# Weight chunks of 128x1024 split in place, and every second modulation chunk multiplied on TensorE in one stage

## The chip, the cores and the metric

The kernel runs on one core of one Trainium2 chip. A core has TensorE (matrix multiplication, PE in the profile; its weight loads are PEld), VectorE (DVE), ScalarE (ACT), GpSimd (POOL) and SyncE (SP), which here only issues DMAs. The engines run side by side and meet at semaphores. The metric is device time in microseconds (us), the median of the runs; lower is better.

## The reference

Two transformer blocks in fp32 for 256 tokens with a width of 2048. Cut to what the change touches:

```python
c_act = silu(c)
mod = c_act @ ada_w + ada_b                   # (2048) @ (2048, 12288): six rows of 2048
sh1, sc1, g1, sh2, sc2, g2 = split(mod, 6)
u = rms_norm(h, norm_mix_g) * (1 + sc1) + sh1
h = h + g1 * hybrid_mixer(u, w_in, ..., w_out)
u = rms_norm(h, norm_ffn_g) * (1 + sc2) + sh2
h = h + g2 * ((silu(u @ w_gate) * (u @ w_up)) @ w_down)
h = rms_norm(h, final_norm_g)
# second block: two layers, each u = h @ w_in_2; pooling or attention; memory attention; @ w_out_2; layer_norm
```

Nearly all the time goes into products of 256 tokens with large weight matrices, and into `c_act @ ada_w`, a product of one row with 100 MB of weights.

## The kernel before

**Stages.** Weights are worked through in stages (`STAGES`, line 72): `memkv`, `ada1`, `win`, `win_end`, attention, `wout`, then `gu0`, `down0`, `gu1` and so on, `in0`, `out0`, `kv`, `in1`, `out1`. A stage has bodies (a loop) of panels. A panel is 512 columns of a matrix, and its 2048 rows are 16 blocks of 128 rows, fetched as 8 chunks of two blocks (512 KB). The kind of a panel says what it fetches: `w` a weight matrix, `a` a slice of `ada_w`, `wa` both in turn. `ada1` has four panels of kind `a`: it fetches only modulation weights, 32 chunks, and its results (shift and gain) are needed before `win` can begin, the first panel of which is of kind `w`.

**A weight block** must keep fp32 accuracy on TensorE, so it is split in two: ScalarE rounds it (`w_hi`, line 338), VectorE subtracts (`w_lo`, line 370), and TensorE does three matmuls of 512 columns for each half of the tokens (lines 444 to 446), 6 in a block, 12 in a chunk. `w_hi` and `w_lo` each have 4 slots of one block (`HILO`).

**A modulation block** is multiplied by its scalars of `c` and added up on VectorE: `ada_acc` = block x `c_col` + `ada_acc` (line 377 for the first block of a panel, 385 for the other 15). Each waits for the one before. When the 16 are done, TensorE adds up the 128 partitions with four fp32 matmuls of one column against `ones` (`ada_sum`, line 402; the profile records eight), and VectorE takes the four columns out of PSUM bank 6 and adds the bias (`take_columns`, line 1479). The take of a panel stands in VectorE's program at block 12 of the panel after it.

**The ring.** SyncE fetches into `raw`, 8 slots of one chunk (`RING`), in order, one DMA each (two in the `gu` stages). Before each fetch it waits for one counter, `blocks_read`, which VectorE raises once a block is subtracted or accumulated. So a slot is free as soon as VectorE has read it, while TensorE may still be up to four blocks behind. SyncE's waits stand in one queue: a fetch whose slot is not free holds up all behind it.

**Order of the other work.** Small steps are hooked into the programs of the engines at block numbers. At the start of some stages (a *lead*) the activations are turned by TensorE (line 483), and for each pair of blocks VectorE scales them (line 551 or 553, `evac`), ScalarE rounds (line 526), VectorE subtracts (line 558, `actT`), between the splits of the weights. In `kv`'s lead GpSimd scales `X` (lines 1080 and 1083, `natural`) beside that. In `wout` and the `down` stages VectorE's hook `gated_add` adds a finished panel to `X`.

Of the kernel before, what the change touches and what calls it, by code (L numbers as in the profile page):

```python
# [56 lines left out]
RING, HILO = 8, 4  # L57
# [6 lines left out]
class Stage:  # L64
# [8 lines left out]
    Stage("memkv", 2, [("wa", 16)] * 2), Stage("ada1", 2, [("a", 16)] * 2),  # L73
# [13 lines left out]

# [5 lines left out]
for _s in STAGES:  # L93
    _s.start = (_kb, _gb, _pn, _an)
    _s.local = []
    k = g = n = a = 0
    for _kind, _nk in _s.panels:
        _s.local.append((k, g, n, a))
        k += _nk * len(_kind)
        g += _nk * ("w" in _kind)  # L100
# [20 lines left out]
def program(nc, x, c, ada_w, ada_b, norm_mix_g, norm_ffn_g, w_in, fox_f_bias, cmp_w1, cmp_w2, cmp_pos,  # L121
# [6 lines left out]
    with ctx:  # L128
# [23 lines left out]
        r_hilo = region(2 * HILO * NC * 4)  # L152
        w_hi = at("w_hi", [P, HILO, NC], f32r, r_hilo)
        w_lo = at("w_lo", [P, HILO, NC], f32r, r_hilo + HILO * NC * 4)
# [95 lines left out]
        blocks_read = S("blocks_read")  # L250
        hi_ready = S("hi_ready")
        parts_used = S("parts_used")
# [5 lines left out]
        def chunks(stage, j):  # L258
# [3 lines left out]
            for ch in range(nk // 2):  # L262
                for k in kind:
                    yield k, ch, off
                    off += 2

        def stage_loads(sp, name, w_src, a_src=None, width=NC):
            st = ST[name]

            def body(p, first):  # L270
                for j in range(len(st.panels)):
                    pl = place(st, p, j)
                    for kind, ch, off in chunks(st, j):
                        slot = ((st.start[0] + st.local[j][0] + off) // 2) % RING

                        sp.wait_ge(blocks_read, pl.kb + off + 2)
# [10 lines left out]
        for st in STAGES:  # L287
# [3 lines left out]
            for j in range(len(st.panels)):  # L291
                row = []
                for kind, ch, off in chunks(st, j):
                    s = ((st.start[0] + st.local[j][0] + off) // 2) % RING
# [18 lines left out]
        def stage_split_hi(act, name, hooks=None, width=None, lead=None):  # L313
# [3 lines left out]
            def body(p, first):  # L317
                for j in range(len(st.panels)):
# [4 lines left out]
                    for idx, (kind, ch, off) in enumerate(chunks(st, j)):  # L323
                        if kind != "w":
                            continue
                        for b in range(2):
                            k = 2 * ch + b
# [4 lines left out]
                            if b == 0:  # L332
                                wait_chunk(act, st, p, j, idx)
                            slot = ((st.start[0] + st.local[j][0] + off) // 2) % RING

                            act.wait_ge(parts_used, pl.gb + k + 1)
                            g = (st.local[j][1] + k) % HILO
                            act.activation(w_hi[:, g, 0:w], raw[:, slot, b, 0:w], ACT.Copy).then_inc(hi_ready, 1)  # L338
            run_bodies(act, st, body)

        def stage_split_lo(dve, name, hooks=None, width=None, take=None, one_acc=False, lead=None):
# [7 lines left out]
            def body(p, first):  # L349
                na = 0  # L350
                for j in range(len(st.panels)):
# [3 lines left out]
                    for idx, (kind, ch, off) in enumerate(chunks(st, j)):  # L355
                        slot = ((st.start[0] + st.local[j][0] + off) // 2) % RING
                        for b in range(2):
                            k = 2 * ch + b
# [7 lines left out]
                            if kind == "w":  # L366

                                dve.wait_ge(hi_ready, pl.gb + k + 1)
                                g = (st.local[j][1] + k) % HILO
                                nc.vector.tensor_tensor(w_lo[:, g, 0:w], raw[:, slot, b, 0:w],  # L370
                                                        w_hi[:, g, 0:w].bitcast(f32),
                                                        ALU.subtract).then_inc(blocks_read, 1)
                            else:
                                acc = ada_acc[:, 0 if one_acc else na % 2, :]
                                if k == 0:
                                    wait_chunk(dve, st, p, j, idx)
                                    nc.vector.tensor_scalar(acc, raw[:, slot, b, :], c_col[:, 0:1], None,
                                                            ALU.mult).then_inc(blocks_read, 1)
                                else:
                                    if b == 0:  # L380
                                        wait_chunk(dve, st, p, j, idx)
# [1488 lines left out]
```

## Time and profile before

| | us |
|---|---|
| median of 3 runs | 2327.52 |
| lowest and highest | 2325.42, 2329.5 |
| span of the profiled execution | 2324.9 |
| TensorE busy | 2105.9 (91%) |
| VectorE busy | 1503.5 (65%) |
| ScalarE busy | 1063.4 (46%) |
| DMA, mean | 209 GB/s |

The profiled execution has its span of 2324.9 us only; what lies around it is the 2.6 us to the median. An x with a number is a count of instructions. A bracket at the end of a row of a timeline tells how long the engine was idle before it, and what released it. PEclk is the clock that TensorE was granted, 1.00 for 2.4 GHz and 0.50 for 1.2 GHz.

### The profile page before, as it was taken

The numbers are of one execution on the slowest core, as the hardware profiler recorded it, in microseconds if no ns is written. First come the engines' busy times: TensorE is split into PE (matmuls) and PEld (weight loads), VectorE is DVE, ScalarE is ACT, GpSimd is POOL, SyncE is SP. The second block draws the span as 40 slices with busy tenths as digits, with TensorE's granted clock in tenths as the row PEclk, the third lists the DMA queues.
The fourth block names the chain that finished last, engine by engine and source line by source line (L and its number), as shares of the span: only waits on it lengthen the run. The fifth ranks groups of instructions, "written<-read, shape, count | busy, mean of one in ns | idle before, by whom it ended". The sixth has DMA issues, their size and how long they took to land.

```text
span 2324.9 us, 29571 instructions
## 1 busy us (share of the span) xinstructions
PE 2105.9 (91%) x9820; PEld 1731.4 (74%) x9820; DVE 1503.5 (65%) x2632; ACT 1063.4 (46%) x1931; POOL 117.8 (5%) x188
## 2 busy tenths in 40 slices
PE   6928999998798999999999999799799699999797
PEld 4817888776576887888888888588578578888675
DVE  5988888656898877555555556755345755555466
ACT  3414444466334544445544554455334445555542
POOL 2000000221003000000000000100000300000000
PEclk9958999999899999999999999899899899999998
DMA  9986998523796997666656665466526356664462
GB/s 299 387 297 230 359 320 312 172 80 89 278 335 203 293 292 244 199 191 190 189 188 194 190 189 186 132 196 193 166 78 226 109 168 194 190 197 138 154 218 99
DMA packets 321589, 486.09 MB, mean 209 GB/s; under 512 B 33696, under 2 KB 145536, under 8 KB 320064
## 3 DMA queue, kind: packets, MB, share of 16 engines
q1 hardware_dynamic: 318704, 468.63, 62.6%
q0 software_dynamic: 2768, 15.98, 1.9%
q8 instruction: 64, 1.05, 0.2%
q14 instruction: 53, 0.43, 0.1%
HBM read 465.13 MB, written 2.10 MB: 201 GB/s over the span
## 4 chain that ended last, share of the span: by engine, by line
PE 75%; DVE 11%; issue 6%; SPq 3%; DMA 2%; ACT 2%; POOL 0%; DVEq 0%; POOLq 0%; ACTq 0%
PE ps L444 23%; PE ps L446 23%; PE ps L445 23%; DVE ada_acc L385 4%; SPq L812 3%; DVE w_lo L370 3%; PE ps L483 1%; PE ps L696 1%; PE ps L659 1%; ACT w_hi L338 1%; DMA raw<-in_w_mem_kv 1%; PE ps L1311 1%; PE ps L643 1%; DVE evac L551 1%; DMA raw<-in_w_out 1%
## 5 line engine op out<-in xcount | busy, mean ns | idle before, releaser
L370 DVE TENSOR_TENSOR w_lo<-raw,w_hi 128x512 fp32r<-128x512 f32 (+1 forms) x1328 | 919.1, 703 | 628.4 <-ACT w_hi L338 626.2
L338 ACT ACTIVATE w_hi<-raw 128x512 fp32r<-128x512 f32 (+1 forms) x1328 | 829.4, 629 | 1004.4 <-PE ps L446 893.0
L444 PE MATMUL ps<-w_hi,actT 128*128 128x512 f32 (+1 forms) x2304 | 915.1, 397 | 60.3 <-DVE actT L558 24.4
L446 PE MATMUL ps<-w_hi,actT 128*128 128x512 f32 (+1 forms) x2304 | 901.7, 391 | 0.0
L445 PE MATMUL ps<-w_lo,actT 128*128 128x512 f32 (+1 forms) x2304 | 901.2, 391 | 0.0
L444 PEld LDWEIGHTS ps<-w_hi,actT 128*128 128x128 f32 x2304 | 437.4, 190 | 162.2 <-DVE actT L558 27.9
L446 PEld LDWEIGHTS ps<-w_hi,actT 128*128 128x128 f32 x2304 | 437.0, 190 | 92.1
L445 PEld LDWEIGHTS ps<-w_lo,actT 128*128 128x128 f32 x2304 | 438.3, 190 | 88.5 <-issue 1.4
L385 DVE SCALAR_TENSOR_TENSOR ada_acc<-raw,c_col,ada_acc 128x512 f32<-128x512 f32 x360 | 271.7, 755 | 11.7 <-DMA raw<-in_ada_w 2.3
L444 PE MATMUL ps<-w_hi,hidT 128*128 128x512 f32 x352 | 137.7, 391 | 2.8 <-DVE w_lo L370 2.8
L446 PE MATMUL ps<-w_hi,hidT 128*128 128x512 f32 x352 | 137.0, 389 | 0.0
L445 PE MATMUL ps<-w_lo,hidT 128*128 128x512 f32 x352 | 137.0, 389 | 0.0
L444 PEld LDWEIGHTS ps<-w_hi,hidT 128*128 128x128 f32 x352 | 66.1, 188 | 18.5 <-DVE w_lo L370 2.6
L446 PEld LDWEIGHTS ps<-w_hi,hidT 128*128 128x128 f32 x352 | 66.1, 188 | 13.9
L445 PEld LDWEIGHTS ps<-w_lo,hidT 128*128 128x128 f32 x352 | 66.1, 188 | 13.4
L402 PE MATMUL ps<-ones,ada_acc 128*128 128x1 f32 x128 | 18.8, 268 | 51.1 <-DVE ada_acc L385 51.1
L696 PE MATMUL ps<-v_s,probsT 128*128 128x64 f32 (+1 forms) x424 | 56.2, 282 | 9.3 <-DVE probsT L788 7.8
L696 PEld LDWEIGHTS ps<-v_s,probsT 128*128 128x128 f32 x424 | 52.7, 198 | 11.7 <-DVE probsT L788 8.6
L402 PEld LDWEIGHTS ps<-ones,ada_acc 128*128 128x128 f32 x128 | 19.6, 225 | 52.3 <-DVE ada_acc L385 51.5
L659 PE MATMUL ps<-qkT_s 64*128 64x256 f32 (+3 forms) x272 | 46.2, 389 | 11.2 <-ACT probs L726 6.1
L726 ACT ACTIVATE probs<-probs,sm 128x128 f32<-128x128 f32 x120 | 52.8, 444 | 4.4 <-DVE sm L776 4.4
L1074 POOL TENSOR_TENSOR rinv_x<-ms,mhalf 128x2 f32<-128x2 f32 x4 | 3.4, 854 | 994.7 <-DVE ms L1511 916.6
(212 smaller groups left out, 1056.6 us busy)
## 6 DMA issues: line engine op xcount, KB each, us to landing
raw<-in_w_in SPq DMA_DIRECT2D x216, 512.0 KB, 4.1
raw<-in_ada_w SPq DMA_DIRECT2D x192, 512.0 KB, 5.6
raw<-in_w_out SPq DMA_DIRECT2D x96, 512.0 KB, 4.9
raw<-in_ffn_w_gate SPq DMA_DIRECT2D x176, 256.0 KB, 2.9
raw<-in_ffn_w_up SPq DMA_DIRECT2D x176, 256.0 KB, 3.1
raw<-in_ffn_w_down SPq DMA_DIRECT2D x88, 512.0 KB, 4.1
raw<-in_w_kv_shared SPq DMA_DIRECT2D x48, 512.0 KB, 3.7
raw<-in_w_mem_kv SPq DMA_DIRECT2D x32, 512.0 KB, 8.8
```

The costliest lines, as they stand in the source:

```text
L338: act.activation(w_hi[:, g, 0:w], raw[:, slot, b, 0:w], ACT.Copy).then_inc(hi_ready, 1)
L370: nc.vector.tensor_tensor(w_lo[:, g, 0:w], raw[:, slot, b, 0:w], w_hi[:, g, 0:w].bitcast(f32), ALU.subtract).then_inc(blocks_read, 1)
L385: nc.vector.scalar_tensor_tensor(acc, raw[:, slot, b, :], c_col[:, k:k + 1], acc, ALU.mult, ALU.add).then_inc(blocks_read, 1)
L402: last = nc.tensor.matmul(ps[:, 6, i:i + 1], acc[:, i * P:(i + 1) * P], ones[:, 0:1], start=True, stop=True)
L444: nc.tensor.matmul(o, hi, w_hi[:, g, 0:w], start=(k == 0), stop=False)
L445: nc.tensor.matmul(o, hi, w_lo[:, g, 0:w], start=False, stop=False)
L446: last = nc.tensor.matmul(o, lo, w_hi[:, g, 0:w], start=False, stop=(k == nk - 1))
L483: last = nc.tensor.transpose(ps[:, 4 + g % 4, i * P:(i + 1) * P], src(k, t), ident[:, :])
L659: last = nc.tensor.matmul(ps[:, 2 + h, c0:c0 + nk], q[:, t * P:(t + 1) * P], k[:, 0:nk], start=True, stop=True)
L696: last = nc.tensor.matmul(o, probsT[:, par, h, d:d + P], self.v(par, h, kt), start=(kt == 0), stop=(kt == nk // P - 1))
L726: last = act.activation(probs[:, par, h, c0:c0 + nk], src, ACT.Exp, bias=sm[:, par, q:q + 1], scale=self.scale, accum_out=sm[:, par, 4 + q ...
L812: sp.dma_start(dst, src[:, t]).then_inc(sem, 16)
```

## The change

The splits are made for a whole chunk, 128x1024, with one instruction on ScalarE and one on VectorE, half as many as before. `w_lo` has no buffer of its own: it is written over the chunk in `raw`. `w_hi` gets the room, and holds 4 chunks (8 blocks) where it held 4 blocks. TensorE waits once in a chunk and frees it once, after its 12 matmuls.

`blocks_read` is replaced by three counters. SyncE now frees a slot by what was in it: a weight chunk when TensorE has done its matmuls (`parts_used`), a modulation chunk when VectorE has accumulated it (`ada_step`) or TensorE has multiplied it (`ada_pe`).

In `ada1` alone the panels become of kind `ap`: chunks 0, 2, 4, 6 go to VectorE as before, chunks 1, 3, 5, 7 to TensorE, where `ada_direct` multiplies the raw fp32 weights with a column of `c` into the four columns of bank 6: eight fp32 matmuls of one column in a chunk. `ada_sum` then adds VectorE's half to the same columns. Because these share the bank, `ada_direct` waits until the panel before was taken (`ada_taken`), and that take still stands in VectorE's program at block 12, so behind chunk 4 of the panel.

```diff
-RING, HILO = 8, 4
+RING, HI = 8, 4
...
-Stage("ada1", 2, [("a", 16)] * 2),
+Stage("ada1", 2, [("ap", 16)] * 2),
...
+        w_lo = at("w_lo", [P, RING, 2, NC], f32r, 0)
+        r_hilo = region(HI * 2 * NC * 4)
+        w_hi = at("w_hi", [P, HI, 2, NC], f32r, r_hilo)
...
+        def slot_free(sp, st, p, first, j, off):
+
+            per = st.per[0]
+            n = st.start[0] + st.local[j][0] + off - RING + (0 if first else per)
+            if n < 0:
+                return
+            kind = loaded[n]
...
+            if kind == "w":
+                sp.wait_ge(parts_used, HI + done)
+            elif kind == "a":
+                sp.wait_ge(ada_step, 2 * done)
+            else:
+                sp.wait_ge(ada_pe, done)
...
-                        sp.wait_ge(blocks_read, pl.kb + off + 2)
+                        slot_free(sp, st, p, first, j, off)
...
-                            act.wait_ge(parts_used, pl.gb + k + 1)
-                            g = (st.local[j][1] + k) % HILO
-                            act.activation(w_hi[:, g, 0:w], raw[:, slot, b, 0:w], ACT.Copy).then_inc(hi_ready, 1)
+                        act.wait_ge(parts_used, pl.gb + ch + 1)
+                        g = (st.local[j][1] + ch) % HI
+                        act.activation(w_hi[:, g, :, 0:w], raw[:, slot, :, 0:w], ACT.Copy).then_inc(hi_ready, 1)
...
+                            nc.vector.tensor_tensor(w_lo[:, slot, :, 0:w], raw[:, slot, :, 0:w],
+                                                    w_hi[:, g, :, 0:w].bitcast(f32),
+                                                    ALU.subtract).then_inc(lo_ready, 1)
...
+        def ada_direct(pe, st, p, j):
+
+            pl = place(st, p, j)
+            pe.wait_ge(ada_taken, pl.an + 1)
+            for idx, (kind, ch, off) in enumerate(chunks(st, j)):
+                if kind != "p":
+                    continue
+                wait_chunk(pe, st, p, j, idx)
+                slot = slot_of(st, j, off)
+                for b in range(2):
+                    k = 2 * ch + b
+                    for i in range(4):
+                        last = nc.tensor.matmul(ps[:, 6, i:i + 1], raw[:, slot, b, i * P:(i + 1) * P], c_col[:, k:k + 1],
+                                                start=(idx == 1 and b == 0 and i == 0), stop=False,
+                                                skip_group_check=True)
+                last.then_inc(ada_pe, 1)
...
+                            if b == 0:
+                                pe.wait_ge(lo_ready, pl.gb + ch + 1)
...
-                            last.then_inc(parts_used, 1)
+                        last.then_inc(parts_used, 1)
```

## Rows read from the trace of the kernel before

**Rows 1.** Busy time by stretch: engine us (x), PEclk, DMA share, GB/s

```profile
55.00:110.00 55.00, 55.00 (x251) 45.57 (x250) 52.45 (x82) 26.97 (x47) 0.00 (x0) 1.00 1.05 387
110.00:165.00 55.00, 16.73 (x82) 14.52 (x81) 47.86 (x76) 9.66 (x16) 1.36 (x2) 0.64 0.88 304
1155.00:1210.00 55.00, 55.00 (x248) 45.54 (x247) 29.70 (x46) 27.14 (x46) 0.00 (x0) 1.00 0.60 191
```

**Rows 2.** Waits: waiter <- waited for: us in total, times, longest

```profile
PE ps L402 <- DVE ada_acc L385: 51.1, 4, 18.7
PE ps L444 <- DVE w_lo L370: 20.4, 20, 3.3
ACT w_hi L338 <- PE ps L446: 893.0, 1155, 7.6
```

**Rows 3.** Timeline, VectorE, ada1: start us, length us, line, tiles, count

```profile
123.11 4.83 DVE L1501 BATCH_NORM_STATS2 stats<-X 128x6 f32<-128x512 f32 x8
129.38 12.25 DVE L385 SCALAR_TENSOR_TENSOR ada_acc<-raw,c_col,ada_acc 128x512 f32<-128x512 f32 x15
```

**Rows 4.** Timeline, TensorE, ada1 and the start of win

```profile
141.68 1.87 PE L402 MATMUL ps<-ones,ada_acc 128*128 128x1 f32 x8 [18.69 <-DVE ada_acc L385]
179.73 1.87 PE L402 MATMUL ps<-ones,ada_acc 128*128 128x1 f32 x8 [10.82 <-DVE ada_acc L385]
187.26 0.77 PE L444 MATMUL ps<-w_hi,actT 128*128 128x512 f32 x1 [1.71 <-issue]
```

**Rows 5.** Line 402 (min/median/max ns), and its eight records in memkv

```profile
L402 PE MATMUL ps<-ones,ada_acc x128: 165/250/373, 64.9 to 471.7; 128*128 128x1 f32 x128
87.61 0.95 PE L402 MATMUL ps<-ones,ada_acc 128*128 128x1 f32 x8
```

**Rows 6.** Thin matmuls in win_end (timeline), and granted clock around their end

```profile
401.27 4.07 PE L1235 MATMUL ps<-cmp_in,w_s 64*64 64x30 f32 x64
...
404.00:405.00 1.00, 1.00 (x20) 1.00 (x19) 0.00 (x0) 0.00 (x0) 0.00 (x0) 0.94 0.55 211
405.00:406.00 1.00, 1.00 (x6) 0.84 (x5) 0.00 (x0) 0.00 (x0) 0.00 (x0) 0.50 0.07 27
```

**Rows 7.** Timeline, memkv in steady state: queue, ScalarE, VectorE

```profile
88.78 1.29 DVE L370 TENSOR_TENSOR w_lo<-raw,w_hi 128x512 fp32r<-128x512 f32 x2
89.99 1.53 DVE L385 SCALAR_TENSOR_TENSOR ada_acc<-raw,c_col,ada_acc 128x512 f32<-128x512 f32 x2
90.10 0.37 SPq L279 DMA_DIRECT2D raw<-in_w_mem_kv  x1
90.82 1.24 ACT L338 ACTIVATE w_hi<-raw 128x512 fp32r<-128x512 f32 x2 [1.54 <-DMA raw<-in_w_mem_kv]
```

**Rows 8.** Page, DMA issues: count, KB each, us from issue to landing

```profile
raw<-in_ffn_w_down SPq DMA_DIRECT2D x88, 512.0 KB, 4.1
raw<-in_w_mem_kv SPq DMA_DIRECT2D x32, 512.0 KB, 8.8
```

**Rows 9.** Groups with shapes kept apart, VectorE

```profile
L1804 DVE TENSOR_TENSOR U<-U 128x1024 f32<-128x1024 f32 x1 | 1.2, 1224 | 0.0
```

**Rows 10.** Timeline, first panel of win: one group of the lead

```profile
199.76 1.29 DVE L370 TENSOR_TENSOR w_lo<-raw,w_hi 128x512 fp32r<-128x512 f32 x2 [0.62 <-ACT w_hi L338]
```

**Rows 11.** Timeline, first panel of kv: VectorE, GpSimd, TensorE

```profile
1844.15 9.84 DVE L370 TENSOR_TENSOR w_lo<-raw,w_hi 128x512 fp32r<-128x512 f32 x2 [0.62 <-ACT w_hi L338]
1848.62 4.82 POOL L1083 TENSOR_TENSOR X<-X,gb 128x2048 f32<-128x2048 f32 x1
1858.96 0.79 PE L444 MATMUL ps<-w_hi,actT 128*128 128x512 f32 x1 [12.35 <-DVE actT L558]
1866.04 0.79 PE L444 MATMUL ps<-w_hi,actT 128*128 128x512 f32 x1 [2.48 <-DVE actT L558]
```

**Rows 12.** Timeline, TensorE: starts of down0, and inside down2

```profile
912.29 0.47 PE L444 MATMUL ps<-w_hi,hidT 128*128 128x512 f32 x1 [1.47 <-DVE w_lo L370]
1426.22 0.50 PE L444 MATMUL ps<-w_hi,hidT 128*128 128x512 f32 x1 [0.45 <-DVE w_lo L370]
```

More of the change, by code:

```diff
@@ L72 @@
 STAGES = [
[L73 removed]
+    Stage("memkv", 2, [("wa", 16)] * 2), Stage("ada1", 2, [("ap", 16)] * 2),
     Stage("win", 2, [("w", 16)] + [("wa", 16)] * 3), Stage("win_end", 1, [("wa", 16), ("w", 16)] * 2),
@@ L262, in chunks, with slot_of @@
             for ch in range(nk // 2):
-                for k in kind:
+                for k in kind[ch % 2] if kind == "ap" else kind:
                     yield k, ch, off
-                    off += 2
+                    off += 1
+        def slot_of(st, j, off):
+            return (st.start[0] + st.local[j][0] + off) % RING
+        loaded = "".join(k for st in STAGES for _ in range(st.bodies)
+                         for j in range(len(st.panels)) for k, _, _ in chunks(st, j))
+        def slot_free(sp, st, p, first, j, off):
[4 more added lines that the diff above has]
+            kind = loaded[n]
+            done = loaded[:n + 1].count(kind)
+            each = sum(k == kind for j2 in range(len(st.panels)) for k, _, _ in chunks(st, j2))
+            done = done if first else done - each + p * each
+            if kind == "w":
[4 more added lines that the diff above has]
+                sp.wait_ge(ada_pe, done)
         def stage_loads(sp, name, w_src, a_src=None, width=NC):
@@ L355, in body @@
                     for idx, (kind, ch, off) in enumerate(chunks(st, j)):
-                        slot = ((st.start[0] + st.local[j][0] + off) // 2) % RING
-                        for b in range(2):
-                            k = 2 * ch + b
+                        slot = slot_of(st, j, off)
+                        for k in (2 * ch, 2 * ch + 1):
                             if not alone and kind == kinds[j][0]:
@@ L396, in ada_sum @@
             kind, nk = st.panels[j]
-            pe.wait_ge(blocks_read, 2 * RING + pl.kb + nk * len(kind))
+            pe.wait_ge(ada_step, steps_before(st, pl) + (KD // 2 if kind == "ap" else KD))
             pe.wait_ge(ada_taken, pl.an + 1)
-            if as_columns:
+            if kind == "ap":
+                for i in range(4):
+                    last = nc.tensor.matmul(ps[:, 6, i:i + 1], acc[:, i * P:(i + 1) * P], ones[:, 0:1],
+                                            start=False, stop=(i == 3), skip_group_check=True)
+            elif as_columns:
                 for i in range(4):
@@ L443, in body @@
                                 o = ps[:, bank + t, 0:w]
[L444 to L447 removed]
+                                nc.tensor.matmul(o, hi, w_hi[:, g, b, 0:w], start=(k == 0), stop=False)
+                                nc.tensor.matmul(o, hi, w_lo[:, slot, b, 0:w], start=False, stop=False)
+                                last = nc.tensor.matmul(o, lo, w_hi[:, g, b, 0:w], start=False, stop=(k == nk - 1))
+                        last.then_inc(parts_used, 1)
             run_bodies(pe, st, body)
```

79 lines of the change are left out of this document (38 added, 41 removed).

## The prediction

> **What bounds the kernel now.** I read busy time by stretch first, then the waits, then the timeline at the places that those name. In `memkv` (55 to 110) TensorE has no gap, at full clock; VectorE is busy for 52.45 of 55 us and the DMAs bring 387 GB/s, so three resources are nearly full together. In the stages of pure weights TensorE has no gap either, and VectorE (29.70) and the DMAs (191 GB/s) have room. From 110 to 165, mostly `ada1`, TensorE is busy for 16.73 us and VectorE for 47.86 [rows 1]. The waits say the same: TensorE's longest is in line 402 for `ada_acc`, 51.1 us in 4 waits; all its waits for `w_lo` come to 20.4 us [rows 2]. So the kernel is bound by TensorE's weight matmuls, except in `ada1`, where VectorE's chain of accumulations sets the end, and in some starts of stages.
>
> **`ada1` before.** VectorE first does the statistics of `x` (from 123.11), then the blocks one behind the other: 15 in 12.25 us, so 0.82 us each [rows 3]. The sums of the four panels stand from 141.68 to 179.73, so 12.68 us for a panel; the last one ends at 181.6, and `win`'s first matmul starts at 187.26 [rows 4].
>
> **`ada1` after: TensorE's chain.** VectorE's part halves: 8 x 0.82 = 6.5 us for a panel. TensorE gets four chunks of eight fp32 matmuls, each chunk twice the work of one sum. A sum of the same form (weights 128x128, one column) is eight records and takes 1.87 us here [rows 4], and 0.95 us in `memkv` [rows 5]; the difference is the clock. Which clock will `ada_direct` see? The nearest row is the run of thin matmuls in `win_end`: 64 records with 30 columns, back to back for 4.07 us, with TensorE counted busy for 1.00 of each us; the granted clock was still 0.94 in their last us and 0.50 in the next one, so that the dense matmuls behind them started at half clock [rows 6]. `ada_direct` has one column, and in front of three of its four panels the clock is low already. I take the low clock throughout, 1.2 GHz. Eight records one after the other take 1.71 us then (1.87 less the tail of the last one, which the next covers: longest record 373 ns [rows 5] less the spacing of 214), so a panel is 8 x 1.71 = 13.7 us, at most 8 x 1.87 = 15.0.
>
> These 13.7 us are in a ring of waits. `ada_direct` of panel j waits for the take of panel j-1; that take waits for the sum of j-1; the sum stands behind `ada_direct` of j-1. So the period is 13.7 + 1.9 (sum) + 0.3 (take, semaphores) = 15.9 us, against 12.68. VectorE and the loads fit under it: chunk 3's slot comes free halfway through `ada_direct` (7 us), chunk 4 lands some 5 us later, VectorE needs 1.6 us: 13.6 of the 15.9. The first panel overlaps with the statistics: TensorE starts it at 123.2 and has done by some 133, VectorE begins its half one block before 129.38 and finishes at 128.9 + 8 x 0.8 = 135.3. For the first take, VectorE must get through chunks 0, 2, 4 of panel 1, which the DMAs at 387 GB/s (1.36 us a chunk) bring by 139.0, so 139.0 + 1.6 + 0.3 = 140.9. Then three periods: the last sum ends at 140.9 + 3 x 15.9 - 0.3 = 188.3, against 181.6: **+6.7 us** (with 15.0 for the direct part: +10.6). Nothing hides it, since `win` needs the result. Behind this SyncE has `win`'s loads, which are due only at 190.
>
> **The larger split.** ScalarE and VectorE do the same elements. 128x1024 takes VectorE 1.224 us [rows 9]; the pair it replaces takes 1.21 from its start to the next instruction's [rows 7]; with the usual overlap of 0.08 the new one takes 1.14. That is 0.07 us in a chunk, of use only where VectorE is the last, in `wout` (32 chunks): -2 to 0; I set it against the ring below. But the first `w_lo` of a chunk now waits for a `w_hi` of twice the length. Where TensorE stands still for it (`down0`, 1.47 us [rows 12], and the starts of `memkv` and `win_end`) that adds 0.5 to 0.6 us each: **+1.6**. In the leads VectorE waits 0.62 us for `w_hi` in every group [rows 10], and this grows to 1.1, so a group takes 0.45 more; over five groups +2.2 at most. Against that, `w_hi` has room for chunk 2 and later ones without waiting for TensorE, which gives a lead of 1 to 2.7 us at its beginning. I take **0** for the leads, -1 to +1.5 for each of four.
>
> **The deeper `w_hi`.** ScalarE waits 893.0 us for TensorE [rows 2]: it is early nearly always, and can now run four chunks ahead. In the stages of pure weights VectorE's hook is then covered: three stalls of 0.45 in `down2` (one in [rows 12]) go, **-1.4**. From 0 to -8 for the rest of the waits for `w_lo` [rows 2]; those in `wout` I expect to stay, since there VectorE or the DMAs are the bound.
>
> **GpSimd beside `kv`'s lead.** Two subtractions take 9.84 us together at 1844.15 and end as GpSimd's long instructions end (1848.62 starts the second); TensorE stands still for 12.35 and later 2.48 us [rows 11]. By these rows each VectorE instruction with two SBUF inputs waits for a boundary on GpSimd. One subtraction in place of two waits for one boundary fewer (4.8 us), but GpSimd's last boundary (1848.62 and three instructions of 4.9, so 1863.3) stays: the chunk after the 2.48 us stall can start at 1863.3 and not at 1866.04: **-2.7**, between -5 and 0. The Trainium skill (SBUF — State Buffer, "SBUF: two separate sides") calls the port pair of the two engines an exclusive lock held for the whole instruction. By that rule fewer and longer instructions lose fewer turns, which agrees with the row.
>
> **Slots freed later.** A `w` slot was freed when `w_lo` was written (90.10 follows 88.78 + 1.29 directly [rows 7]); now it stays until TensorE has done the chunk, at least 2.7 us more, and the modulation fetch behind it in SyncE's queue waits too. Of the four `w` slots in a `wa` panel each goes round once in 4 x 2.72 = 10.9 us: load + `w_hi` 1.2 + `w_lo` 1.2 + matmuls 2.7 + semaphores 0.3 = load + 5.4. It holds if a load takes up to 5.5 us. Loads take 4.1 us where the DMAs have room, 8.8 in `memkv` [rows 8], where six of them queue; fewer in flight also land sooner. Two fetches issued together give about 4.1 + 1.36 = 5.5, just the limit. Bounds 0 and +27 (8.8 us in 32 chunks: (14.2 - 10.9) / 4 = 0.83 each); I take +1, nearest to 4.1, and with the faster VectorE **0**.
>
> **Sum.** +6.7 + 1.6 - 1.4 - 2.7 + 0 = +4.2 us. The profiled span of 2324.9 becomes 2329.1, and with the 2.6 us around it the median of 2327.5 becomes 2331.7: **2332 us**.
>
> **A rule against it, and the rivals.** The Trainium skill (TensorE: Matmul & The Clock Gate, "Why this matters for your kernels") advises to keep TensorE busy without gaps to get and keep the full clock. By this rule the direct matmuls, which leave no gap, bring it to full clock; the thin matmuls of `win_end` speak against it.
>
> *Rival 1, the full clock in `ada1`* (22%). A chunk takes 16 x 0.12 = 1.9 us, a panel 7.6, a sum 0.95 [rows 5]. TensorE's ring is then 8.9 us, and the loads bind: 8 x 1.36 = 10.8, some 11 us for a panel. The first panel after the statistics has a low start (9.5 us), so the last sum ends near 172.4: -9.2 in place of +6.7. The start of `win`, at half clock now, saves 2.4 us as well. 4.2 - 15.9 - 2.4 = -14: 2313 us.
>
> *Rival 2, the ring starves* (13%), slower. It decides from a load of 5.5 us on: then `wa` stages run at the pace of the ring, with TensorE waiting for `w_lo` and ScalarE for DMAs. Up to +27 in `memkv`; half of it gives 2345.
>
> *Rival 3, the queue absorbs more* (10%): half of the 20.4 us of waits for `w_lo` goes: 2332 - 10 = 2322.
>
> *Rival 4, the engines don't share `ada1`*: that is within my forecast, since the take at block 12 makes TensorE wait for chunk 4 of the next panel.
>
> **How the numbers follow.** The forecast has 55%, with 2326 to 2339 as its own range (direct part of 15.0 us, GpSimd at 0, leads). Cases of both signs are likely, so the range reaches to rivals 1 and 2: 2311 to 2345. A measurement of this kernel can tell about 0.2% from no change, 4.7 us. Faster: rival 1 (21), rival 3 (6), the forecast's edge (3): 30%. Within: half of the forecast, and 4 of rival 3: 31%. Slower: the rest, 39%.
>
> **What would show it.** In the profile after: PEclk of 0.5 through `ada1`, sums 15.9 us apart, eight thin records in 1.7 us, first matmul of `win` near 194. In `memkv` still 12 matmuls in 2.72 us without gaps and w loads of 5 to 6 us. In `kv`'s lead one stall of TensorE shorter by 3 to 5 us. The forecast is wrong if the clock is high in `ada1`, or if TensorE waits for `w_lo` in `wa` panels.

## The result, and the profile after

| | before | changed |
|---|---|---|
| median of the runs, us | 2327.99 | 2345.74 |
| ratio | 1 | 1.0079, 95% interval 1.006 to 1.0098 |
| the same measured again | 2323.74 | 2341.87, ratio 1.0067, 1.005 to 1.0084 |
| span of the profiled execution | 2324.9 | 2344.8 (again: 2341.9) |

The change costs about 18 us (17.75 and 18.13 between the medians). 2332 was forecast, and 2345.74 lies just outside the range of 2311 to 2345. The four times behind it reach from 2336.14 to 2347.37, and the second measurement, 2341.87, lies inside the range; so what counts is not the edge but the size of the loss, four times the forecast +4.2.

To see where a loss arises I cut the profiled executions at marks that every kernel has: TensorE's first weight matmul, the sums of `ada_sum`, the turning of the activations. The stretches, each the difference of two starts in TensorE's timeline (us):

| | to the first matmul | `memkv`: to its last sum | `ada1`: to its last sum | `win`, attention: to the turning for `wout` | `wout`: to the turning of `xn` | to `kv`'s turning | to the end | span |
|---|---|---|---|---|---|---|---|---|
| before | 27.5 | 94.5 | 57.7 | 414.1 | 127.2 | 1105.2 | 498.6 | 2324.9 |
| changed | 29.0 | 103.1 | 65.0 | 411.7 | 130.3 | 1108.7 | 497.0 | 2344.8 |
| changed, again | 28.6 | 101.7 | 65.2 | 415.4 | 127.9 | 1106.4 | 496.7 | 2341.9 |

Two stages carry the loss: `memkv` with 7.2 to 8.6 us and `ada1` with 7.3 to 7.5.

**`memkv`.** Busy time by stretch, changed kernel; columns as in [rows 1]:

```profile
core 0: us, PE busy (x) PEld busy (x) DVE busy (x) ACT busy (x) POOL busy (x), PEclk, DMA share, GB/s
55.00:110.00 55.00, 49.60 (x216) 40.46 (x215) 46.81 (x57) 21.02 (x22) 0.00 (x0) 0.94 0.99 354
1155.00:1210.00 55.00, 55.00 (x249) 45.54 (x248) 24.80 (x26) 20.66 (x25) 0.00 (x0) 1.00 0.60 190
```

Against [rows 1], TensorE and VectorE have lost their full use (5.4 us of gaps, 5.6 us less of VectorE's work), and the DMAs bring 354 in place of 387 GB/s. None of the engines is full there any more: they wait for one another. The stages of pure weights are as full as before, with less work on VectorE (24.80 in place of 29.70) and ScalarE. The waits of the changed kernel (waiter <- waited for: us in total, times, longest), to be read beside [rows 2]:

```profile
PE ps L496 <- DVE w_lo L389: 24.6, 15, 4.7
ACT w_hi L358 <- PE ps L498: 530.8, 348, 5.7
ACT w_hi L358 <- DMA raw<-in_w_mem_kv: 72.2, 32, 11.9
DVE ada_acc L404 <- DMA raw<-in_ada_w: 24.2, 17, 4.5
```

ScalarE waited 42.0 us for the `memkv` weights before and waits 72.2 now. The one long stall, in the timelines of SyncE's queue, ScalarE and TensorE (start, length, ..., idle before it and what ended it):

```profile
55.26 0.37 SPq L301 DMA_DIRECT2D raw<-in_w_mem_kv  x1
57.87 0.37 SPq L303 DMA_DIRECT2D raw<-in_ada_w  x1
65.16 0.37 SPq L301 DMA_DIRECT2D raw<-in_w_mem_kv  x1
57.47 1.06 ACT L358 ACTIVATE w_hi<-raw 128x1024 fp32r<-128x1024 f32 x1 [7.62 <-DMA raw<-in_w_mem_kv]
59.92 0.77 PE L496 MATMUL ps<-w_hi,actT 128*128 128x512 f32 x1 [4.70 <-DVE w_lo L389]
```

A chunk arrives late, TensorE stands still for 4.70 us, and since a weight slot is freed by TensorE now, SyncE issues nothing from 57.87 to 65.16. That pause itself makes no second stall: the chunk issued at 65.16 lands at 68.8, and TensorE reaches it at 74.0. What the stall costs beside its own length is the clock: it falls to 0.50 meanwhile (rows in the last section), so that the 12 matmuls behind it take 5.05 us in place of 2.72. Those 2.3 us, the 4.70 and two later gaps (0.70 and 0.36) are 8.1 of the 8.6 us. What made the chunk late shows in the DMAs' view of 44 to 60 us (out<-in, queue, count, KB each, median us from issue to landing):

```profile
raw<-in_w_mem_kv SPq DMA_DIRECT2D x5, 512.0 KB, 10.3
X<-in_x POOLq DMA_DIRECT2D x1, 2048.0 KB, 11.2
```

GpSimd fetches `x` then, 2 MB in one go, at 44.90. It did so before the change too (at 43.62); then nobody stalled. The difference is how far the ring was ahead. The first weight fetch behind that of `x` in SyncE's queue, before the change and changed:

```profile
44.16 0.37 SPq L279 DMA_DIRECT2D raw<-in_w_mem_kv  x1
47.10 0.37 SPq L301 DMA_DIRECT2D raw<-in_w_mem_kv  x1
```

When `x` is issued, TensorE is at the fifth weight chunk in both. The first row is the fetch of the tenth chunk, so four were under way or there ahead of `x`; the second is that of the ninth, so three were. Before the change the chunk lands at 55.2 and TensorE starts it at 56.6 without a gap. In the changed kernel it lands at 57.4, when TensorE has had no work since 55.2, and the split in whole chunks then takes 2.5 us up to the first matmul, where 1.4 were enough.

**`ada1`.** TensorE's timeline, beside [rows 4]:

```profile
132.10 0.95 PE L451 MATMUL ps<-ones,ada_acc 128*128 128x1 f32 x8
133.30 11.03 PE L432 MATMUL ps<-c_col,raw 128*128 128x1 f32 x64 [0.25 <-DVE modT L1531]
145.17 1.87 PE L447 MATMUL ps<-ones,ada_acc 128*128 128x1 f32 x8 [0.83 <-DVE ada_acc L404]
151.91 13.81 PE L432 MATMUL ps<-c_col,raw 128*128 128x1 f32 x64 [4.87 <-DVE modT L1531]
165.58 1.85 PE L447 MATMUL ps<-ones,ada_acc 128*128 128x1 f32 x8
181.36 1.84 PE L447 MATMUL ps<-ones,ada_acc 128*128 128x1 f32 x8
183.46 13.81 PE L432 MATMUL ps<-c_col,raw 128*128 128x1 f32 x64 [0.25 <-DVE modT L1531]
197.13 1.84 PE L447 MATMUL ps<-ones,ada_acc 128*128 128x1 f32 x8
204.50 0.77 PE L496 MATMUL ps<-w_hi,actT 128*128 128x512 f32 x1 [1.57 <-issue]
```

The 64 one-column records of a panel take 13.81 us, the sums stand 15.8 us apart (12.7 before), and once the first take is over TensorE is the engine that hardly rests (0.25 us in a period). The first panel takes less, 11.03 us, since it starts at full clock; the clock falls in the middle of it, while TensorE has no gap:

```profile
134.00:136.00 2.00, 2.00 (x20) 2.00 (x20) 2.00 (x4) 0.00 (x0) 0.00 (x0) 1.00 1.05 394
138.00:140.00 2.00, 2.00 (x11) 2.00 (x11) 1.83 (x7) 0.00 (x0) 0.90 (x2) 0.50 0.00 0
```

**What got better.** In `win_end` five stalls for `w_lo` of 0.39 to 0.75 us (2.6 us together) are gone, and so are the three of 0.45 in `down2` (one of 0.22 is left); TensorE's two stalls in `kv`'s lead are 1.5 us shorter together. The stretches `win` with attention and up to `kv`'s turning scatter between kernels with the same code there (405 to 415 and 1105 to 1109, table below), and of the kernel before there is one profile; so nothing smaller is read from them.

### The profile page after: what moved, and what is told of

It reads as the page before. It is cut to its first block, busy times and chain, and to the rows that moved or that the text cites. A ratio compares the mean times of both kernels' runs of the same rounds, so it can differ in the third digit from the quotient of the medians.

```text
span 2344.8 us, 28052 instructions
## 1 busy us (share of the span) xinstructions
PE 2166.8 (92%) x10076; PEld 1791.4 (76%) x10076; DVE 1389.3 (59%) x1936; ACT 930.9 (40%) x1267; POOL 122.2 (5%) x188
## 4 chain that ended last, share of the span: by engine, by line
PE 75%; DVE 8%; issue 7%; DMA 4%; SPq 3%; ACT 3%; POOL 0%; DVEq 0%; POOLq 0%; ACTq 0%
PE ps L496 22%; PE ps L498 22%; PE ps L497 22%; SPq L864 2%; PE ps L432 2%; DMA raw<-in_w_mem_kv 2%; DVE w_lo L389 2%; DVE ada_acc L404 1%; ACT w_hi L358 1%; PE ps L748 1%; PE ps L711 1%; DMA raw<-in_w_out 1%; DVE evac L603 1%; PE ps L695 1%; PE ps L1363 1%
## 5 line engine op out<-in xcount | busy, mean ns | idle before, releaser
L389 DVE TENSOR_TENSOR w_lo<-raw,w_hi 128x1024 fp32r<-128x1024 f32 (+1 forms) x664 | 817.4, 1239 | 556.5 <-ACT w_hi L358 554.7
L358 ACT ACTIVATE w_hi<-raw 128x1024 fp32r<-128x1024 f32 (+1 forms) x664 | 694.7, 1054 | 888.3 <-PE ps L498 530.8
L404 DVE SCALAR_TENSOR_TENSOR ada_acc<-raw,c_col,ada_acc 128x512 f32<-128x512 f32 x328 | 247.0, 753 | 30.7 <-DMA raw<-in_ada_w 24.2
L497 PEld LDWEIGHTS ps<-w_lo,hidT 128*128 128x128 f32 x352 | 66.1, 188 | 13.5
L1819 DVE TENSOR_TENSOR hidT<-ps,hidT 128x512 f32 (+1 forms) x22 | 15.2, 690 | 100.6 <-ACT hidT L1480 100.6
L748 PEld LDWEIGHTS ps<-v_s,probsT 128*128 128x128 f32 x424 | 53.9, 201 | 12.9 <-DVE probsT L840 9.3
L1480 ACT ACTIVATE hidT<-ps 128x512 f32 (+1 forms) x22 | 13.1, 597 | 121.3 <-PE ps L1323 121.3
L432 PE MATMUL ps<-c_col,raw 128*128 128x1 f32 x256 | 52.5, 341 | 5.6 <-DVE modT L1531 5.6
L432 PEld LDWEIGHTS ps<-c_col,raw 128*128 128x128 f32 x256 | 52.1, 317 | 6.0 <-DVE modT L1531 6.0
```

The costliest lines, as they stand in the source:

```text
L358: act.activation(w_hi[:, g, :, 0:w], raw[:, slot, :, 0:w], ACT.Copy).then_inc(hi_ready, 1)
L389: nc.vector.tensor_tensor(w_lo[:, slot, :, 0:w], raw[:, slot, :, 0:w], w_hi[:, g, :, 0:w].bitcast(f32), ALU.subtract).then_inc(lo_ready, 1)
L404: nc.vector.scalar_tensor_tensor(acc, raw[:, slot, k % 2, :], c_col[:, k:k + 1], acc, ALU.mult, ALU.add).then_inc(ada_step, 1)
L432: last = nc.tensor.matmul(ps[:, 6, i:i + 1], raw[:, slot, b, i * P:(i + 1) * P], c_col[:, k:k + 1], start=(idx == 1 and b == 0 and i == 0) ...
L497: nc.tensor.matmul(o, hi, w_lo[:, slot, b, 0:w], start=False, stop=False)
L748: last = nc.tensor.matmul(o, probsT[:, par, h, d:d + P], self.v(par, h, kt), start=(kt == 0), stop=(kt == nk // P - 1))
```

## The experiments

What a kernel leaves out stands in its expectation. The stretches of all are in one table at the end of this section; ratios are to the kernel before, measured beside each.

**1. Taking the change apart.** First `ada1` alone undone:

```diff
-Stage("ada1", 2, [("ap", 16)] * 2),
+Stage("ada1", 2, [("a", 16)] * 2),
```

> The changed kernel, but the four panels of ada1 are accumulated by VectorE alone again. The output is the reference's. Theory (ring): the 19 us come in two parts that have nothing to do with each other: the ring of slots, mostly in memkv, and the half-clocked chain of TensorE in ada1. So here the last sum of memkv still starts near 132 us (122.2 in the kernel before), ada1 is back at sums 12.7 us apart, the stretch from that sum to the end of ada1's last sum is 59.4 us again and not 66.9, and the time is 2345.7 - 7.5 = 2338 us. Rival: ada1 took its loss over from memkv (the slots that TensorE's chain holds, the clock); then the stretch stays above 63 us and the time above 2342.

Measured: 2333.46 us, ratio 1.0032 (1.0021 to 1.0042). TensorE's timeline:

```profile
147.84 1.87 PE L447 MATMUL ps<-ones,ada_acc 128*128 128x1 f32 x8 [18.70 <-DVE ada_acc L404]
160.53 1.87 PE L447 MATMUL ps<-ones,ada_acc 128*128 128x1 f32 x8 [10.82 <-DVE ada_acc L404]
```

`ada1` takes 57.7 us again, to a tenth as before, while `memkv` still takes 100.3. The two losses are independent. The time fell below the expected 2338; in its profile `memkv` and `win` with attention are shorter than in the first one of the change.

**2. Slots freed early, in the old room.** A separate `w_lo` of two chunks and a `w_hi` of two:

```diff
-RING, HI = 8, 4
+RING, HI = 8, 2
...
-                sp.wait_ge(parts_used, HI + done)
+                sp.wait_ge(lo_ready, done)
```

> The changed kernel, but w_lo has a buffer of its own again (two chunks, and w_hi two chunks, so together the room of the kernel before), and a slot of the ring is free as soon as VectorE has subtracted from it. The splits stay 128x1024, ada1 stays shared. The output is the reference's. Theory (slots held by TensorE starve the ring): memkv's last sum starts at 122 to 125 us in place of 132, TensorE's stalls of 4.7 us in memkv and of 3.4 and 4.7 us in wout shrink to those of the kernel before, ada1 still costs its 7.5 us, the three 0.45 us stalls in down2 come back: 2345.7 - 9 - 3 + 1 = 2335 us. Rival (the coarser split itself, one wait for 1024 columns, makes memkv late): the last sum stays near 132, and the time at 2345 or above.

> Both edits together: slots freed by VectorE, ada1 on VectorE alone; what is left of the change is the 128x1024 split alone. The output is the reference's. Theory: the two parts add up, 2335 - 7.5 = 2327 to 2328 us, the kernel before within 0.2%. Rival (the coarser split makes memkv late): 2338.

> Control for the run with the early freed slots: the changed kernel with w_lo written in place and slots held until TensorE is done, but w_hi only two chunks deep in place of four. The output is the reference's. Theory: the depth of w_hi matters little, 2346 to 2349 us, memkv's last sum still near 132. Rival (the deeper w_hi of the changed kernel lets ScalarE run ahead and takes slots or turns from the others): memkv gets faster here, and the time falls below 2342.

Measured: 2398.07 us, ratio 1.0306 (1.0293 to 1.0319), for the first; 1.0268 (1.0254 to 1.0281) with `ada1` on VectorE; 1.0331 (1.0316 to 1.0346) for the control with slots held. All three expectations of the time are far off, for a reason that the control shows: with whole chunks, a `w_hi` of two chunks costs some 60 us over the whole kernel. ScalarE and VectorE of the control at 1170 us:

```profile
1169.96 1.06 ACT L358 ACTIVATE w_hi<-raw 128x1024 fp32r<-128x1024 f32 x1 [1.68 <-PE ps L498]
1171.05 1.23 DVE L389 TENSOR_TENSOR w_lo<-raw,w_hi 128x1024 fp32r<-128x1024 f32 x1 [0.85 <-ACT w_hi L358]
1172.71 1.06 ACT L358 ACTIVATE w_hi<-raw 128x1024 fp32r<-128x1024 f32 x1 [1.69 <-PE ps L498]
```

ScalarE may start only when TensorE has done a whole chunk, and then 1.06 + 1.23 us and the semaphores must fit under the one other chunk (2.72 us): nothing is left for any other step of the two engines. Even this undisturbed round takes 2.75. So the changed kernel's four chunks of `w_hi` are no luxury; they are what the coarser split needs. The comparison of early and held slots points the way, and no more: 1.0306 against 1.0331, which is 5.8 us, with intervals that touch, and `memkv` takes 97.7 and 96.7 us against 100.8, where held slots alone scatter from 98.1 to 103.1 (below).

**3. Slots freed early, with the full depth.** In `memkv`, and then in `wout` too, `w_lo` goes into four chunks of memory that these stages leave free:

```diff
+        EARLY = ('memkv',)          # then ('memkv', 'wout')
+        w_lo2 = at("w_lo2", [P, HI, 2, NC], f32r, r_one)
...
+                if owner.name in EARLY:
+                    sp.wait_ge(lo_ready, done)
```

> The changed kernel with w_hi four chunks deep, but in memkv alone w_lo goes into a buffer of its own of four chunks (in memory that memkv leaves free), and a weight slot of memkv is free once VectorE has subtracted. Everything else as changed. The output is the reference's. Theory (held slots starve the ring): from memkv's first matmul to its last sum 95 to 97 us in place of 103.1 (before: 94.7), the stall of 4.7 us gone, time 2345.7 - 7 = 2339. Rival (the 128x1024 split makes memkv late by itself): 100 us or more, time above 2343.

> As the run with the early freed slots in memkv, and the same in wout. The output is the reference's. Theory: wout (turning of X to turning of xn) takes 127.5 us as before the change and not 130.3, and with memkv's 7 us the time is 2336. Rival: wout stays at 130 because VectorE, with its gated adds, is late there; then 2339.

Measured: 2329.58 us, ratio 1.0037 (1.0022 to 1.0052), and 2324.28 us, ratio 1.0007 (0.9995 to 1.0019). `memkv` takes 93.7 and 94.3 us, a little less than before the change, where the nine profiles with held slots (eight with four chunks of `w_hi`, one with two) have 98.1 to 103.1. Both times lie below the expected 2339 and 2336; by the ratios the first gains 7 to 10 us on the changed kernel (7 were expected) and the second 14 to 17. SyncE's queue at the same place, and the stretch:

```profile
54.30 0.37 SPq L307 DMA_DIRECT2D raw<-in_w_mem_kv  x1
56.94 0.37 SPq L309 DMA_DIRECT2D raw<-in_ada_w  x1
58.98 0.37 SPq L307 DMA_DIRECT2D raw<-in_w_mem_kv  x1
55.00:110.00 55.00, 55.00 (x253) 45.83 (x252) 50.55 (x61) 23.94 (x26) 0.00 (x0) 1.00 1.05 387
```

When `x` is issued, at 44.22, six weight chunks are ahead of TensorE's. The 7.3 us without an issue are gone, TensorE has no gap, and the DMAs are back at 387 GB/s, although the fetch of `x` is where it was. That settles `memkv`: it is the late freeing; the larger split costs nothing there once slots come free early. (`w_lo` has a buffer of its own in these kernels as well, and no run frees late with such a buffer; but a subtraction takes 1.23 us in both forms.) In `wout` the stretch falls to 123.2 us (123.3 and 123.3 in two more runs, below), where it is 127.9 to 131.3 with held slots and 127.2 before the change: neither the expected 127.5 nor the rival's 130. There the larger split with its deeper `w_hi` does gain, and holding the slots took about all of that gain back, or more. TensorE's waits for `w_lo` from 590 to 742 us are 12.9 us before, 13.9 in the changed kernel and 9.5 here.

**4. The fetch of `x`, later.**

```diff
+            pool.wait_ge(parts_used, HI + 20)
             pool.dma_start(X[:, :, :], x[0].rearrange("(t p) n -> p t n", p=P)).then_inc(S("x_in"), 16)
```

> The changed kernel, but GpSimd's fetch of x (2 MB) is issued only when TensorE is through 20 of memkv's 32 chunks, near 100 us and not near 45. The output is the reference's. Theory (the ring has no room left in memkv, and the DMAs move 387 GB/s at most): 2 MB take 5.4 us of the DMAs wherever they stand, so the stall of 4.7 us at 60 turns up behind 100, and memkv's 103 us stay, time 2344 to 2347. Rival (only the meeting of that fetch with the start of memkv, where the ring is still being filled, makes the stall): memkv 97 to 99 us, time 2340.

Measured: 2338.23 us, ratio 1.0046 (1.0031 to 1.0062). TensorE's only long stall in `memkv`:

```profile
103.89 0.47 PE L496 MATMUL ps<-w_hi,actT 128*128 128x512 f32 x1 [3.59 <-DVE w_lo L389]
```

The stall at 60 us is gone and stands at 104 now: it moves with the fetch (issued at 89.13), so that fetch is its trigger. Again three weight chunks are ahead of TensorE when it is issued. `memkv` takes 99.7 us, inside the 98.1 to 103.1 of the kernels that fetch `x` early, so the stall isn't avoided by moving it. The time came out nearer to the rival's 2340, by `memkv`'s 2 to 3 us and by small differences elsewhere that the place of this fetch doesn't explain; the intervals of this kernel and of the repeated changed one (1.005 to 1.0084) overlap.

**5. TensorE's share of `ada1`.** Two chunks of eight, and two PSUM banks in turn; and the half again, with the two banks alone:

```diff
-                for k in kind[ch % 2] if kind == "ap" else kind:
+                for k in ("p" if ch % 4 == 3 else "a") if kind == "ap" else kind:
...
-            pe.wait_ge(ada_taken, pl.an + 1)
+            pe.wait_ge(ada_taken, pl.an)
...
-                        last = nc.tensor.matmul(ps[:, 6, i:i + 1], raw[:, slot, b, i * P:(i + 1) * P], c_col[:, k:k + 1],
+                        last = nc.tensor.matmul(ps[:, 5 + j, i:i + 1], raw[:, slot, b, i * P:(i + 1) * P], c_col[:, k:k + 1],
```

> The changed kernel, but TensorE gets two of the eight chunks of an ada1 panel (3 and 7) in place of four, and the panels alternate between PSUM banks 5 and 6, so that the direct matmuls wait for no take. The output is the reference's. Theory (ada1 is bound by TensorE at half clock): TensorE now needs 6.9 + 1.9 = 8.8 us for a panel, VectorE 12 x 0.82 + 0.3 = 10.1, the loads 10.8, so the sums stand some 11 us apart (15.8 now, 12.7 before); last memkv sum to last ada1 sum's end 52 to 54 us in place of 66.9; time 2345.7 - 14 = 2332. Rival (shared slots and DMAs make the shared form slow, whatever the share): sums 13 to 16 us apart, time above 2338.

> The changed kernel with half of ada1 on TensorE, but its panels in PSUM banks 5 and 6 in turn, so that the direct matmuls of a panel wait for no take. The output is the reference's. Theory (TensorE itself is the bound, 13.8 us of one-column records and 1.9 us of sum): sums 15.7 us apart in place of 15.8, time unchanged, 2345. Rival (the wait for the take sets the period): sums 11 to 13 apart, 2335.

Measured for the quarter: 2326.69 us, ratio 1.0014 (1.0002 to 1.0027); `ada1` 51.0 us in place of 65.0. TensorE:

```profile
157.23 1.84 PE L447 MATMUL ps<-ones,ada_acc 128*128 128x1 f32 x8
159.27 3.54 PE L432 MATMUL ps<-c_col,raw 128*128 128x1 f32 x16 [0.19 <-DMA raw<-in_ada_w]
164.59 3.58 PE L432 MATMUL ps<-c_col,raw 128*128 128x1 f32 x16 [1.78 <-DMA raw<-in_ada_w]
168.03 1.84 PE L447 MATMUL ps<-ones,ada_acc 128*128 128x1 f32 x8
```

The sums are 11.5, 10.8 and 12.4 us apart, and TensorE waits for DMAs, which bring 381 GB/s from 145 to 170 us: the loads are the bound, as expected (in the last panel it waits 3.32 us for one chunk; why, stays open). The time is below the expected 2332. For the half with two banks (one time, 2331.74 us):

```profile
142.73 1.84 PE L447 MATMUL ps<-ones,ada_acc 128*128 128x1 f32 x8
158.09 1.84 PE L447 MATMUL ps<-ones,ada_acc 128*128 128x1 f32 x8
173.45 1.84 PE L447 MATMUL ps<-ones,ada_acc 128*128 128x1 f32 x8
```

Sums 15.4 apart: the period is TensorE's own, the wait for the take is 0.4 of the 15.8. But the stage takes 59.2 us and not 65.0, against my expectation of no change: I had looked at the period alone, and the wait for the first take (4.87 us in front of the second panel's matmuls in the changed kernel) goes as well. So of the 7.3 us that `ada1` lost, 5.8 (65.0 - 59.2) are the ring through the take, by one profile of each. The other 1.5 are three periods of 15.36 in place of 12.68 (+8.0) less an earlier first sum (13.1 us behind `memkv`'s last one in place of 19.6: -6.5).

**6. The clock.** A modulation block as the moving operand, in TensorE's half of `ada1`:

```diff
-                    for i in range(4):
-                        last = nc.tensor.matmul(ps[:, 6, i:i + 1], raw[:, slot, b, i * P:(i + 1) * P], c_col[:, k:k + 1],
+                    last = nc.tensor.matmul(ps[0:1, 5, :], c_col[:, k:k + 1], raw[:, slot, b, :],
```

> The changed kernel, but a modulation block of TensorE's share goes through as the wide operand: one fp32 matmul with the column of c as its weights and the 512 columns of the block moving, into a row of bank 5, in place of four one-column ones. Left out: that row is not used, so shift and gain lack TensorE's half. Theory (the one-column records don't raise the clock, wide ones do): the granted clock in ada1 goes to 1.0, a block takes 4 x 0.21 = 0.85 us, a chunk 1.7 in place of 3.4; sums 11 us apart, time some 15 us less, 2331. Rival (the clock stays low whatever the form, because the engine rested before): clock 0.5, a block 1.7 us, sums 15.8 apart, time 2345.

> The wide form (a modulation block as the moving operand) without the wait for the take, since its row lies in bank 5. Left out as before: that row is not used, so shift and gain lack TensorE's half. In the first run of this form the clock rose to 1.0, but sums stood 13.9 apart, with TensorE waiting 3.8 us for the take. Theory (with the full clock the ring of the take is the bound): without that wait the loads bind, 8 x 1.36 = 10.8 us, sums 11 us apart. Rival (held slots and loads are the bound): still above 13.

Measured, one time each: 2328.16 us, and 2313.93 without the wait for the take. Stretches of the changed kernel, and of this form without that wait:

```profile
150.00:160.00 10.00, 8.09 (x38) 8.09 (x39) 4.31 (x7) 0.00 (x0) 0.00 (x0) 0.50 0.78 277
185.00:195.00 10.00, 10.00 (x49) 10.00 (x49) 0.00 (x0) 2.11 (x2) 0.00 (x0) 0.50 0.72 242
```

```profile
142.00:144.00 2.00, 2.00 (x3) 0.25 (x2) 1.38 (x2) 0.00 (x0) 0.00 (x0) 0.50 1.04 390
146.00:148.00 2.00, 2.00 (x7) 0.29 (x4) 0.89 (x3) 0.00 (x0) 0.00 (x0) 1.00 1.05 388
150.00:160.00 10.00, 7.81 (x23) 1.80 (x21) 5.42 (x9) 0.00 (x0) 0.00 (x0) 1.00 1.05 386
151.19 1.05 PE L444 MATMUL ps<-ones,ada_acc 128*128 128x1 f32 x8
154.81 1.88 PE L430 MATMUL ps<-raw,c_col 128*1 128x512 f32 x4 [0.75 <-DMA raw<-in_ada_w]
162.01 1.05 PE L444 MATMUL ps<-ones,ada_acc 128*128 128x1 f32 x8
```

With the same weights and a TensorE that is busy in both: with one-column records, which leave no gap from 185 to 195, the granted clock is 0.50; with 512 columns it is 1.00, even with gaps. Nor is this a high clock left over from `memkv`: it is 0.50 at 142 to 144 us and rises while the wide matmuls run. A chunk then takes 1.88 us and a sum 1.05. With the wait for the take the last three sums stood 13.9 and 14.1 us apart; in this row of that run TensorE waits 3.75 us for it:

```profile
164.87 9.15 PE L431 MATMUL ps<-raw,c_col 128*1 128x512 f32 x16 [3.75 <-DVE modT L1529]
```

In that run the clock falls in these waits too (0.58 from 165 to 170 us), so that a panel's 16 records take 9.15 us and not four times 1.88. Without the wait the sums are 10.8 apart, which is the loads' 8 x 1.35 us. This is the situation of my first rival, and its 11 us for a panel hold only once the take is out of the way.

**7. Together.** Early slots in `memkv` and `wout`, a quarter of `ada1` on TensorE, two banks; and the changed kernel once more as a control.

> What the runs so far point to, put together: the changed kernel with early freed slots in memkv and wout (w_lo in a buffer of its own there), two of eight chunks on TensorE in ada1, and its panels in two PSUM banks. The output is the reference's. Theory: the parts add up; the run with early slots in both stages stood at 1.0007 of the kernel before, and ada1 from the last memkv sum to its own last sum took 65.1 us there and 51.0 in the run with a quarter on TensorE: 14.1 us less, 2309 us, ratio 0.995. Rival (the quarter's p chunks and win's loads compete, so the gain is taken back in win's start or later): ratio above 0.998.

> The combined version once more on the same chip as the changed kernel, to compare the two directly: ratio to the kernel before 0.993 to 0.996, memkv 93 to 95 us, ada1 (last memkv sum to its own last sum) 50 to 51 us. Were its gain chance, it would be above 0.998.

> The changed kernel itself once more, as a control. Its first profile has 103.1 us from memkv's first matmul to its last sum, but the seven experiments with the same code in memkv show 98.1 to 101.2, where the two with early freed slots there show 93.7 and 94.3. Theory (held slots cost some 6 us there, and the other 2 to 3 were chance): 98 to 101 us now, a ratio of 1.005 to 1.008. Rival (the first profile is typical, and something in the other kernels shortens memkv): 103 again, ratio 1.008 or more.

Measured: 2313.38 us, ratio 0.9937 (0.9924 to 0.995); again 2312.40, ratio 0.9949 (0.9932 to 0.9966), with `ada1` at 49.2 us, a little below the 50 to 51 expected. The changed kernel again: 2341.87, 1.0067. On the same chip the combined version is 11.3 us faster than the kernel before and 29.5 faster than the changed one. The repeated changed kernel has 101.7 us in `memkv`, a little over the theory's 98 to 101: 98 to 103 is the scatter with held slots.

| | `memkv` | `ada1` | `win`, attention | `wout` | to `kv`'s turning | to the end | span |
|---|---|---|---|---|---|---|---|
| `ada1` on VectorE | 100.3 | 57.7 | 405.9 | 130.5 | 1108.9 | 497.0 | 2328.2 |
| early, two and two chunks | 97.7 | 65.3 | 423.8 | 133.5 | 1137.2 | 504.4 | 2391.2 |
| the same, `ada1` on VectorE | 96.7 | 57.7 | 429.3 | 131.7 | 1140.7 | 505.9 | 2390.2 |
| held, two chunks of `w_hi` | 100.8 | 65.0 | 429.4 | 136.8 | 1136.9 | 506.0 | 2403.3 |
| early in `memkv` | 93.7 | 64.8 | 406.3 | 131.0 | 1108.5 | 496.8 | 2329.8 |
| early in `memkv`, `wout` | 94.3 | 65.1 | 407.2 | 123.2 | 1107.3 | 495.4 | 2321.2 |
| quarter, two banks | 100.5 | 51.0 | 407.5 | 129.7 | 1104.9 | 496.6 | 2319.1 |
| half, two banks | 100.2 | 59.2 | 405.7 | 129.4 | 1109.2 | 496.8 | 2330.0 |
| wide form | 101.0 | 58.5 | 405.3 | 130.6 | 1105.4 | 497.0 | 2326.4 |
| wide form, no take | 98.1 | 46.0 | 406.1 | 131.3 | 1105.4 | 496.6 | 2312.2 |
| `x` later | 99.7 | 64.5 | 411.2 | 130.0 | 1105.9 | 498.2 | 2338.0 |
| combined | 93.1 | 49.8 | 411.0 | 123.3 | 1109.0 | 496.6 | 2311.3 |
| combined, again | 93.1 | 49.2 | 407.3 | 123.3 | 1106.4 | 496.9 | 2305.4 |

## Why the prediction was wrong, step by step

**`ada1`: right.** Low clock in three panels of four (the first starts at full clock and loses it), 13.7 us of one-column records (13.81 measured), a period of 15.9 (15.77), +6.7 us (+7.3 to 7.5). The reading that carried it was [rows 6], the thin matmuls of `win_end`, which said that the clock would stay low. The Trainium skill (TensorE: Matmul & The Clock Gate, "Why this matters for your kernels") advises to keep TensorE busy to get the full clock; the rows of experiment 6 agree for the wide form and disagree for the one-column form, where a TensorE counted busy for the whole of 185 to 195 us stays at 0.50.

**Slots freed later: this step failed.** I took 0 here, between 0 and +27. It is 7.2 to 8.6 us in `memkv`, and 4.7 to 8 in `wout` (127.9 to 131.3 against 123.2), where the larger split with the deeper `w_hi` gains 4.0 (127.2 to 123.2). The working went wrong in two places. It compared a steady load time with a limit of 5.5 us. In the steady part that was nearly enough: in the changed kernel the landings fell from a median of 8.8 us to 5.8 (5.4 from 62 to 115 us), and TensorE has one gap of 0.70 in that stretch. What the old ring also did was to absorb a disturbance. The 2 MB fetch of `x` had no place in the prediction, and it decides: with three weight chunks ahead of it in place of four, and a split that takes some 1 us longer to its first matmul, TensorE stands still for 4.70 us behind it and then runs 12 matmuls at the low clock. And in `wout` I set a gain of 0 to 2 us against a cost of the ring that I never worked out; the runs show 4.0 against 4.7 to 8. (`x` is fetched again in `wout`, at 632.52, and the longest stall there, 4.68 us, ends at 648.36; that the fetch is the trigger there too is not shown.) The rival was there, "the ring starves", at 13% and with TensorE waiting for `w_lo` in `wa` panels as its mark, as it came. But it had the whole stage at the pace of the ring, and what came is one long stall. Its 2345 is my 2332 with half of a bound of 27; `memkv` lost 7.2 to 8.6 and not 13.5, so that the time agrees with it is in part luck.

**First `w_lo` waits longer: right in size, where the wait is one.** `down0`'s stall grew from 1.47 us [rows 12] to 2.01, and `win_end`'s first one from 0.94 to 1.48:

```profile
933.23 0.47 PE L496 MATMUL ps<-w_hi,hidT 128*128 128x512 f32 x1 [2.01 <-DVE w_lo L389]
```

`memkv`'s first matmul came 1.1 to 1.5 us later (0.5 expected). But it waits for `actT` before and after the change, so it isn't shown that this is the larger split's doing.

**Deeper `w_hi`: right where it was costed, and more.** The three stalls of 0.45 in `down2` went but for 0.22, and 2.6 us in `win_end` besides. What I had not seen is that the depth is needed (experiment 2).

**GpSimd beside `kv`'s lead: -2.7 forecast, -1.5 measured** (-1.2 in the repeated run). TensorE and GpSimd there, beside [rows 11]:

```profile
1876.18 0.80 PE L496 MATMUL ps<-w_hi,actT 128*128 128x512 f32 x1 [8.00 <-DVE actT L610]
1886.61 0.80 PE L496 MATMUL ps<-w_hi,actT 128*128 128x512 f32 x1 [5.36 <-DVE actT L610]
1870.21 5.37 POOL L1135 TENSOR_TENSOR X<-X,gb 128x2048 f32<-128x2048 f32 x1
1880.61 5.38 POOL L1135 TENSOR_TENSOR X<-X,gb 128x2048 f32<-128x2048 f32 x1
```

One boundary fewer is waited for (8.00 in place of 12.35 us), but the second stall grew from 2.48 to 5.36: GpSimd's four instructions now take 20.4 us in place of 19.4, two of them being longer beside VectorE's longer ones (5.37 in place of 4.82 and 5.38 in place of 4.89), and `actT` still waits for the last of them.

**Leads at 0**: `win`'s is 1.8 us shorter up to the first sum (60.5 to 58.7 us), 0.8 beyond the -1 that I gave a lead. Why the stretches of `win` with attention and up to `kv`'s turning scatter by 10 and 4 us between executions stays open.

**The sum.** With the profile of the repeated run: +1.1 (first matmul) + 7.2 (`memkv`) + 7.5 (`ada1`) + 1.3 (`win`, attention) + 0.7 (`wout`) + 1.2 - 1.9 (end) = 17.0, the difference of the spans (terms rounded). Forecast were 4.2. The largest part of the difference is `memkv`'s 7.2, which stood in the sum at 0.

## What to carry to other kernels

Ask of a ring of buffers not only whether its round fits the load time, but what reserve it keeps for the largest other transfer of the stage; a stall of the engine that sets the pace can cost more than its own length, here 7 us for 4.7, by the clock that it loses. Don't let a slot wait for the engine that is the bound when another has finished with it earlier. When work is moved to an idle engine, share it by the slowest of all the partners, the DMAs among them (here a quarter, not a half), and look for the wait that ties two panels together before the rates.

## What was not expected of the hardware

- One-column fp32 matmuls, 128x128 weights each, back to back for 13.81 us leave the granted clock at 0.50; fp32 matmuls of 512 columns against one column of weights bring it to 1.00 in the same stage and keep it there with TensorE busy for 7.81 of 10 us. Back-to-back one-column records don't keep a full clock either: it fell in the middle of 11.03 us of them. At full clock both forms cost about the same for a chunk: 1.88 us wide, and 1.92 us for the 16 one-column records of the first chunk in the quarter's run, before the clock fell.
- In a stall of 4.70 us the clock fell from full to half, so that the first ten matmuls after it stand some 0.43 us apart in place of 0.23. Busy time and clock of two stretches, changed kernel:

```profile
58.00:60.00 2.00, 0.07 (x1) 0.10 (x1) 1.45 (x2) 0.52 (x1) 0.00 (x0) 0.50 1.05 397
62.00:64.00 2.00, 2.00 (x6) 1.52 (x6) 1.96 (x4) 1.14 (x2) 0.00 (x0) 0.50 1.03 391
```

- Two of GpSimd's four 128x2048 products got longer (5.37 in place of 4.82 us the first of them) when VectorE's instructions beside them doubled in length; the other two kept their 4.57 and 5.0 us. The Trainium skill (SBUF — State Buffer, "SBUF: two separate sides") has the lock block whichever engine comes second; the rows agree, in both directions: a subtraction of 1.23 us takes 5.47 beside GpSimd's products.
